# Even mixer of a two-block network: pool products in the first attention step, four output slots woven into the attention, a room of its own for the fourth one's weights

## What is computed

```python
def even_mixer(h, w_in, w_out, q_g, k_g, pool_w, pool_scale):
    proj = h @ w_in
    q, k, v, qi, ki, wi, u = jnp.split(proj, offsets, axis=-1)
    q = rms_norm_2(q.reshape(b, t, A_HEADS, HEAD_DIM), q_g)
    k = rms_norm_2(k.reshape(b, t, A_KV_HEADS, HEAD_DIM), k_g)
    attn = dsa_attention(q, k, v, qi, ki, wi)      # 8 heads, each query sees 64 chosen keys
    pooled = multiscale_pool(u, pool_w, pool_scale)
    return jnp.concatenate([attn, pooled], axis=-1) @ w_out

def multiscale_pool(u, pool_w, pool_scale):        # 4 groups of 128 features, windows 2, 4, 8, 16
    for g, w in enumerate(POOL_WINDOWS):
        outs.append((hi - lo) / count - groups[:, :, g])   # mean of the last w tokens, less the token
    y = jnp.einsum('btgc,gcd->btgd', mixed, pool_w)
    return y * pool_scale
```

## Time and profile before

| | |
|---|---|
| median of 3 runs | 1366.63 us (1365.58 to 1368.62) |
| the profiled execution's own time | 1366.33 us |
| its span, first to last instruction | 1364.5 us |
| PE busy | 1313.2 us, 96% of the span |
| PE weight load, DVE, ACT, POOL busy | 1262.1, 667.7, 676.8, 1017.6 us |
| mean granted clock of TensorE | 0.990 |
| share of PE in the chain that ended last | 79% |

### The profile page before, as it was taken

The page is one execution under the profiler, slowest core; times in us unless marked ns, Lnnn a source line. Parts: engine busy times, 40 slices in busy tenths (PEclk is TensorE's granted clock), DMA queues, the critical chain, the costliest instruction groups (busy, mean ns, idle before and its releaser), DMA issues.

```text
span 1364.5 us, 27769 instructions
## 1 busy us (share of the span) xinstructions
PE 1313.2 (96%) x11024; PEld 1262.1 (92%) x11024; DVE 667.7 (49%) x1168; ACT 676.8 (50%) x933; POOL 1017.6 (75%) x794
## 2 busy tenths in 40 slices
PE   7989999999999989999999979999999999999999
PEld 6879999999988889999999858999999998999999
DVE  8994465555556757555566484211113545211112
ACT  7715543444666656444456545444445445544442
POOL 1226898888777549888887775988887764888885
PEclk9989999999999989999999989999999999999999
DMA  6313675555544334555554532555554432555530
GB/s 261 125 63 126 180 245 186 183 179 180 167 149 161 110 108 163 185 184 180 179 178 144 186 123 68 208 180 179 181 179 159 152 124 93 173 189 181 180 141 31
DMA packets 33879, 217.07 MB, mean 159 GB/s; under 512 B 3683, under 2 KB 7428, under 8 KB 8196
## 3 DMA queue, kind: packets, MB, share of 16 engines
q1 hardware_dynamic: 30096, 211.14, 43.9%
q10 hardware_dynamic: 3700, 4.75, 1.4%
HBM read 213.26 MB, written 2.62 MB: 158 GB/s over the span
## 4 chain that ended last, share of the span: by engine, by line
PE 79%; DVE 11%; ACT 4%; issue 2%; POOL 2%; DMA 1%; DVEq 0%; ACTq 0%; SPq 0%; POOLq 0%
PE up L1481 18%; PE up L1482 17%; PE up L1483 17%; PE acc L1481 6%; PE acc L1483 6%; PE acc L1482 6%; PE up L1601 2%; POOL w_lo L380 1%; ACT w_hi L461 1%; DVE opnd L877 1%; DVE s_work L1017 1%; DVE mix L886 1%; PE side L1687 1%; DVE s_work L1026 1%; DVE mix L1359 0%
## 5 line engine op out<-in xcount | busy, mean ns | idle before, releaser
L380 POOL TENSOR_TENSOR w_lo<-ring,w_hi 128x512 fp32r<-128x512 f32 x756 | 974.0, 1322 | 241.4 <-ACT w_hi L461 238.4
L1481 PE MATMUL up<-opnd,w_hi 128*128 128x256 f32 x2128 | 613.7, 288 | 12.6 <-DVE opnd L1401 3.1
L1482 PE MATMUL up<-opnd,w_lo 128*128 128x256 f32 x2128 | 604.0, 284 | 0.0
L1483 PE MATMUL up<-opnd,w_hi 128*128 128x256 f32 x2128 | 603.9, 284 | 0.0
L461 ACT ACTIVATE w_hi<-ring 128x2048 fp32r<-128x2048 f32 x191 | 364.6, 1910 | 263.7 <-PE up L1483 210.0
L1481 PEld LDWEIGHTS up<-opnd,w_hi 128*128 128x128 f32 x2128 | 409.7, 193 | 26.8 <-issue 20.1
L1482 PEld LDWEIGHTS up<-opnd,w_lo 128*128 128x128 f32 x2128 | 410.2, 193 | 1.3 <-issue 1.0
L1483 PEld LDWEIGHTS up<-opnd,w_hi 128*128 128x128 f32 x2128 | 410.1, 193 | 0.0
L1481 PE MATMUL acc<-opnd,w_hi 128*128 128x256 f32 x768 | 218.4, 284 | 2.5 <-DVE opnd L1118 2.5
L1482 PE MATMUL acc<-opnd,w_lo 128*128 128x256 f32 x768 | 218.0, 284 | 0.0
L1483 PE MATMUL acc<-opnd,w_hi 128*128 128x256 f32 x768 | 218.0, 284 | 0.0
(11 more groups left out here) (267 smaller groups left out, 1396.0 us busy)
## 6 DMA issues: line engine op xcount, KB each, us to landing
ring<-in_stream SPq DMA_DIRECT2D x197, 1024.0 KB, 4.8
bias_rows<-mix ACTq DMA_DIRECT2D x1, 1536.0 KB
mix<-in_s_b SPq DMA_DIRECT2D x1, 1024.0 KB, 5.6
...
```

Of the source, the lines that this page charges most:

```text
L380: ins = nc.gpsimd.tensor_tensor(w_l[:, cols], ring[:, r, cols], w_h[:, cols].bitcast(f32), ALU.subtract)
L1481: MM(o, l_hi, r_hi, start=start, stop=False, skip_group_check=True)
L1482: MM(o, l_lo, r_hi, start=False, stop=False, skip_group_check=True)
L1483: return MM(o, l_hi, r_lo, start=False, stop=stop, skip_group_check=True)
```

## The change

- The negated pool weights `e_pwn` are written once by ACT. PE multiplies them with u in step 0, as soon as u is there, and adds the products of the weights with the means (sum x 1/count) in the same banks: pool_w x (mean - u) is formed in PSUM. POOL's subtraction L441 goes, and each of its four multiplications tells PE that it is done. The second part of the products stands in step 0 too, in place of step 2.
- ACT and DVE make the pieces 4 to 7 of the operand in step 1 (before: step 3 on ACT, steps 3 and 4 on DVE).
- `fill` starts in step 2 and holds all four slots. The fourth slot uses bank 0 of `acc` once all scores are read: its pieces 4 to 7 in steps 9 and 10, 0 to 3 at the end of step 12. `slot_part` looks up the weights' places, `residual` takes a table of banks.
- The fourth slot's weights get other places in `mix`: over the index vectors and raw queries (high) and over u (low). ACT writes the high part in step 4 (before: step 9), and that of output slot 2 behind the first exponentials (before: ahead of the loop).

```diff
--- before.py
+++ after.py
@@ -295,8 +295,8 @@
         (k_k, k_q, k_v, k_mask, k_tri, k_z, k_t, k_b, k_a, k_out) = carve(
             (KT, T), (KT, T), (TT, D), (384,), (P,), (3, 768), (2, 768), (2, 768), (2, 768), (2, T))
 
-        last_hi = {START["wo"] + 3: mix_r[:, 0:2048], START["evout"] + 3: mix_r[:, 512:2560]}
-        last_lo = {START["wo"] + 3: mix_r[:, 6144:8192], START["evout"] + 3: mix_r[:, 2560:4608]}
+        last_hi = {START["wo"] + 3: mix_r[:, 0:2048], START["evout"] + 3: mix_r[:, 1536:3584]}
+        last_lo = {START["wo"] + 3: mix_r[:, 6144:8192], START["evout"] + 3: mix_r[:, 11984:14032]}
 
         def weights_hi(s):
 
@@ -305,6 +305,8 @@
         def weights_lo(s):
 
             return last_lo[s] if s in last_lo else w_lo[:, s % SPLIT]
+
+        e_pwn = e_at[:, 0].rearrange("p (g d) -> p g d", g=4)
 
         def heads(v):
 
@@ -436,9 +438,7 @@
             pool.wait_ge(dma["causal"], 48)
             for g in range(4):
                 c.up(nc.gpsimd.tensor_tensor(e_cnt[:, g], e_cnt[:, g], (e_pa if g % 2 else e_pb)[:, g, 16:], ALU.mult),
-                     "pool_step")
-            pool.wait_ge(sem("pool_step"), c.of("pool_step").value())
-            c.up(nc.gpsimd.tensor_tensor(e_cnt, e_cnt, e_u[:, :, 16:], ALU.subtract), "pooled")
+                     "pooled")
             low_parts(START["evout"], N_SLOTS)
 
 
@@ -455,7 +455,7 @@
                 if s == START["wo"] + 3:
                     act.wait_ge(sem("diff_scores"), HEADS)
                 elif s == START["evout"] + 3:
-                    act.wait_ge(sem("scores"), 8)
+                    act.wait_ge(sem("qk_ready"), 8 + 3)
                 elif s >= START["glu"] + SPLIT:
                     act.wait_ge(sem("mm_done"), dyn * RING + (s - SPLIT + 1))
                 c.up(A(weights_hi(s), ring[:, s % RING], ACT.Copy), "w_hi_ready")
@@ -806,14 +806,15 @@
             index_relu(0)
             high_parts_to(S + 5)
             index_relu(1)
+            act.wait_ge(dma["causal"], 48)
+            c.up(A(e_pwn, e_pw, ACT.Copy, scale=-1.0), "pool_neg")
             high_parts_to(S + 8)
             even_square(1)
             even_root(1)
             even_square(2)
-            high_parts_to(S + 9)
             for n in range(EVEN_STEPS):
-                if n == 3:
-                    c.wait("pool_ps", 4)
+                if n == 1:
+                    c.wait("pool_ps")
                     for m in range(4):
                         c.up(A(hi("mixed")[:, 4 + m], up[(BANK["evout"] + m // 2) % 2][:, m % 2], ACT.Copy,
                                scale=pcol("pscale", m, 1)), "hi_ready")
@@ -821,13 +822,15 @@
                     even_probs_copy(n - 2)
                 if n < 8:
                     softmax_exp(n, e_l, e_st)
+                if n == 0:
+                    high_parts_to(S + 9)
                 if n == 1:
                     even_root(2)
                 if n >= 5 and n % 2:
                     h = (n - 5) // 2
                     c.wait("pv")
                     c.up(A(hi("mixed")[:, h], aux[h % 2][:, 0:T], ACT.Copy), "hi_ready")
-                if n == 9:
+                if n == 4:
                     high_parts_to(S + 10)
             residual("ffn2", START["evout"], lead=3)
 
@@ -1182,12 +1185,12 @@
                 low_tile(end, 7)
                 c.tell("mix_free")
 
-            def residual(name, S, u0, third=None):
+            def residual(name, S, u0, own={}):
                 for g in range(4):
                     dve.wait_ge(sem("mm_done"), S + g + 1)
                     for e in range(2):
                         m = 2 * g + e
-                        o = third[:, e * T:e * T + T] if third is not None and g == 2 else up[(u0 + g) % 2][:, e]
+                        o = own[g][:, e * T:e * T + T] if g in own else up[(u0 + g) % 2][:, e]
                         c.up_and_wait(V.tensor_tensor(x[:, m], x[:, m], o, ALU.add), "x_ready")
                     c.tell("up_free")
                     for e in range(2):
@@ -1305,7 +1308,7 @@
                     c.wait("hi_ready")
                     c.up(V.scalar_tensor_tensor(lo("diff")[:, h], sq[:, h], sub_g, hi("diff")[:, h].bitcast(f32),
                                                 ALU.mult, ALU.subtract), "lo_ready")
-            residual("ffn1", START["wo"], BANK["wo"], acc[:, 3])
+            residual("ffn1", START["wo"], BANK["wo"], {2: acc[:, 3]})
 
             pe_operand()
             ffn(1, "ple1")
@@ -1395,9 +1398,9 @@
                     softmax_tail(n - 1, e_l, e_a, e_st, False)
                 if n == 2:
                     even_normed(2)
-                if n in (3, 4):
-                    c.wait("hi_ready", 2)
-                    for m in (2 * n - 6, 2 * n - 5):
+                if n == 1:
+                    c.wait("hi_ready", 4)
+                    for m in range(4):
                         c.up(V.scalar_tensor_tensor(lo("mixed")[:, 4 + m], up[(BANK["evout"] + m // 2) % 2][:, m % 2],
                                                     pcol("pscale", m, 1), hi("mixed")[:, 4 + m].bitcast(f32),
                                                     ALU.mult, ALU.subtract), "lo_ready")
@@ -1406,7 +1409,7 @@
                     c.wait("hi_ready")
                     c.up(V.tensor_tensor(lo("mixed")[:, h], aux[h % 2][:, 0:T], hi("mixed")[:, h].bitcast(f32),
                                          ALU.subtract), "lo_ready")
-            residual("ffn2", START["evout"], BANK["evout"], acc[:, 3])
+            residual("ffn2", START["evout"], BANK["evout"], {2: acc[:, 3], 3: acc[:, 0]})
 
             ffn(2, "odd")
             c.tell("mix_free")
@@ -1537,14 +1540,14 @@
 
             def slot_part(name, s, o, ks, fresh=True, order=range(KT)):
 
-                b = s % SPLIT
+                w_h, w_l = weights_hi(s), weights_lo(s)
                 for k in ks:
                     if fresh:
                         c.wait("hi_ready")
                         c.wait("lo_ready")
                     for m in range(2):
                         w = slice((2 * k + m) * P, (2 * k + m + 1) * P)
-                        ins = three(o[:, m], w_hi[:, b, w], w_lo[:, b, w], hi(name)[:, k], lo(name)[:, k],
+                        ins = three(o[:, m], w_h[:, w], w_l[:, w], hi(name)[:, k], lo(name)[:, k],
                                     k == order[0] and m == 0, k == order[-1])
                 if ks[-1] == order[-1]:
                     c.up(ins, "mm_done")
@@ -1963,9 +1966,19 @@
                 c.up(ins, "pv")
 
             out = START["evout"]
-            fill = {4: [(0, [4, 5])], 5: [(0, [6, 7])], 6: [(1, [4, 5])], 7: [(1, [6, 7])], 8: [(0, [0]), (1, [0])],
-                    9: [(2, [4, 5, 6, 7])], 10: [(0, [1]), (1, [1]), (2, [0, 1])], 11: [(0, [2]), (1, [2]), (2, [2])],
-                    12: [(0, [3]), (1, [3]), (2, [3])]}
+            fill = {2: [(0, [4, 5, 6, 7])], 3: [(1, [4, 5])], 4: [(1, [6, 7])], 5: [(2, [4, 5])], 6: [(2, [6, 7])],
+                    7: [(0, [0]), (1, [0]), (2, [0])], 9: [(0, [1]), (1, [1]), (2, [1]), (3, [4, 5])],
+                    10: [(3, [6, 7])], 11: [(0, [2]), (1, [2]), (2, [2])],
+                    12: [(0, [3]), (1, [3]), (2, [3]), (3, [0, 1, 2, 3])]}
+            banks = {}
+
+            def pool_part(weights, v, first):
+
+                for m in range(4):
+                    ins = MM(banks[m // 2][:, m % 2], weights[:, m], v(m), start=(first and m % 2 == 0), stop=not first,
+                             skip_group_check=True)
+                return ins
+
             for n in range(EVEN_STEPS):
                 if n < 8:
                     even_scores(n)
@@ -1976,21 +1989,24 @@
                             pe.wait_ge(sem("lo_ready"), KT * UNIT["mixed"] + 2 * g + 2)
                         if g == 2:
                             used[0] += 1
-                            banks.append(acc[:, 3].rearrange("p (a t) -> p a t", a=2))
+                            banks[g] = acc[:, 3].rearrange("p (a t) -> p a t", a=2)
+                        if g == 3:
+                            used[0] += 1
+                            pe.wait_ge(sem("scores_read"), 8)
+                            banks[g] = acc[:, 0].rearrange("p (a t) -> p a t", a=2)
                     slot_part("mixed", out + g, banks[g], ks, fresh=(g == 0), order=MIXED_ORDER)
                 if n == 0:
+                    banks = {0: bank(), 1: bank()}
+                    pe.wait_ge(sem("pool_in"), 2)
+                    c.wait("pool_neg")
+                    pool_part(e_pwn, lambda m: e_u[:, m, 16:], True)
                     even_stats(2)
+                    c.wait("pooled", 4)
+                    c.up(pool_part(e_pw, lambda m: e_cnt[:, m], False), "pool_ps")
                 if 2 <= n < 10:
                     even_transposes(n - 2)
                 if 4 <= n <= 10 and n % 2 == 0:
                     even_values((n - 4) // 2)
-                if n == 2:
-                    banks = [bank(), bank()]
```

(5 more changed lines are left out.)

## The result

| | before | changed |
|---|---|---|
| median of 7 runs each, side by side | 1364.70 us | 1369.10 us (1368.69 to 1370.80) |
| ratio, 95% interval | | 1.0027 (1.0017 to 1.0037) |
| the profiled execution, its span | 1366.33, 1364.5 us | 1368.78, 1367.0 us |

The change costs 3.7 us by the ratio (2.3 to 5.0 by its interval), more than the 0.2% that can be told from nothing. The forecast was +4.2 us and 1370.5 us. (The base alone covers the 1.4 us between 1370.5 and 1369.1: the forecast started from 1366.33, and the median of the seven runs beside the changed kernel is 1364.70.) The ratios here are of fast runs alone; one run of the kernel before, beside e1, e3, e4 and e5, took 1937.97 us at a granted clock of 0.606 and is in none of them.

A forecast was written before the change was run, and what follows sets the result against it. PE is 96% busy, but a chain off PE sets ffn2's start at T0 + 9.4 us. Terms 2.9 + 1.7 + 0.35 - 2.4 = +2.55 us for T0, +4.25 with the clock behind it: 1370.5 us, range 1365.5 to 1374.

The forecast's parts named there:

- T0: Moment when output slot 0 is complete, 835.5 in the earlier trace; forecast to move +2.55 us, to about 838.
- chain from T0 to ffn2: Additions, operand tiles, ACT's high part and POOL's low part fix ffn2's start at T0 + 9.4 us, whatever PE does.
- Paid in full: Work moved ahead of T0 on PE costs its whole time; work behind T0 is free.
- Term 1: 24 of the fourth slot's 48 matmuls move ahead of T0: +2.9 us; PE then stands still about 4.9 us before ffn2.
- Term 2: Input term on PE, four more fp32 products in step 0: +1.7 us; POOL's dropped 2.69 us released nobody in time.
- Terms 3 and 4: PE's waits from scores 0 to the first pieces, then on to T0: 8.5 us for 8.15, +0.35 us.
- The wait of 3.2 us: PE's first pieces of slot 0 wait for the first low part of the pooled tiles, from 801.3 to 804.5.
- Term 5: POOL's low part of the fourth slot blocks DVE's tails 4 and 5; without it T0 would come about 1 us earlier.
- Rival D: Tails 4 and 5 blocked more, PE feels 2 us, low clock behind T0 twice as long: about 1374; chance 0.13.
- Term 6: Clock ahead of T0: one low stretch costing 0.9 us replaces two costing 3.3, so -2.4 us.
- Term 7: Clock behind T0: a low stretch on ffn2's first slot after PE's 4.9 us gap, +1.7 us (bounds 0 and 3.3).
- C: Rival: DVE catches up in steps 1 to 7 as POOL finishes low parts 2.7 us sooner; 1363.5, chance 0.09.

The follow-up runs named there:

- e1: Changed kernel with all eight pieces of the fourth output slot at the end of step 12, none in steps 9 and 10; ratio 0.9997 to the kernel before.
- e3: Kernel before, with a bank of its own for the fourth output slot and no work moved; ratio 1.0003 to the kernel before.
- e4: e3 plus own places for the weights of ffn2's first slot, converted during the attention; ratio 0.9983 to the kernel before.
- e5: Changed kernel plus own places for the weights of ffn2's first slot, converted in step 9; ratio 0.9991 to the kernel before.
- e11: e9 with the input term on PE, negated products in step 0, pooled ones in step 1, no POOL subtraction; ratio 0.9964 to the kernel before.
- e2: Changed kernel with the input term back on POOL, four pool products in step 0 instead of eight; ratio 1.0002 to the kernel before.
- e6: e1 with ACT writing the fourth slot's high part in step 8 instead of step 4; ratio 0.9978 to the kernel before.
- e9: Changed kernel with input term on POOL, products in step 1, pieces spread thinner, fourth slot last, its high part in step 8; ratio 0.9963 to kernel before.
- e8: e9 plus own places for the weights of ffn2's first slot, high part in step 9; ratio 0.9956 to the kernel before.
- e12: e8 with the high parts of the fourth slot and ffn2's first slot in steps 6 and 8, not 8 and 9; 1356.89 us, ratio 0.9937.

## Why the prediction was right, point by point

- **What bounds the section** was read rightly. The chain from T0 to ffn2 has kept its length (9.30, 9.23 us), and removing the bank's wait is worth nothing (e3). When the chain is cut, ffn2 moves forward (e4, e5). "Paid in full" was too strong: work ahead of T0 that fills a wait is paid in part (terms 1 and 2) or not at all (e11).
- **Term 1, the fourth slot's matmuls**: predicted +2.9 and a gap of about 4.9 us; the gap is 4.96. e1 undoes it and wins 1.9 us at T0. It was 1 us too high, as the pieces also cover 0.75 us of another wait.
- **Term 2, the input term**: predicted 1.7 us on PE. The products take 1.8 us from start to start (791.78 to 793.58). Scores 1 are 5.30 us behind scores 0 and were 2.56, so 2.74 later; predicted 2.7. But the step counted the whole term as the price of having it on PE. With it on POOL (e2) 1.0 of the 1.8 is spent waiting.
- **Terms 3 and 4, the waits**: predicted 8.5 us in all. Measured 0.32 + 0.80 + 2.93 + 0.27 + 1.35 + 0.84 + 1.25 = 7.76. The wait of 3.2 us came with 2.93, those in front of k = 0, transposes 6 and k = 1 with 1.35, 0.84 and 1.25. The wait of scores 4 for the logits did not come; transposes 4 waited 0.27 us in its place.
- **Term 5, DVE under POOL**: right; 1.4, 1.2 and 1.3 us for three operations, about 1.5 us of PE's path (e6). Rival D's trigger was there; its price, 2 us more than the forecast, wasn't.
- **Term 6, the clock ahead of T0, is the step that failed in the profiled run.** Predicted -2.4 us: one low stretch of 3.3 us, partly over a wait. The low stretches of the changed kernel, against the earlier trace rows (the last one is ffn2's first slot):

```profile
799.80:806.60 6.80, 5.42 (x25) 5.45 (x26) 6.62 (x11) 0.95 (x2) 6.55 (x6) 0.50 0.56 202
827.10:830.50 3.40, 3.40 (x16) 3.40 (x17) 0.00 (x0) 0.00 (x0) 0.00 (x0) 0.50 0.02 5
847.60:851.00 3.40, 3.40 (x18) 3.40 (x18) 3.03 (x5) 2.64 (x6) 3.40 (x3) 0.50 0.69 234
```

  The clock fell while PE still stood in the gap of 2.93 us and stayed low for 6.8 us, 5.4 of them over PE's work. The 24 matmuls of slot 0 took 806.44 - 801.18 = 5.26 us instead of 2.9. A second stretch followed at 827.1. In these two PE lost 2.4 us and 0.44 x 3.4 = 1.5, together 3.9. The two of before (the windows of the earlier trace rows start up to 0.7 us late; the stretches themselves, at a clock of 0.50, run from 801.0 to 804.4 and from 811.3 to 814.7) lost 1.4 on the pool products (3.19 us for what takes 1.8 in the changed kernel) and 1.5, together 2.9. So it is about +1.0 in the place of -2.4, and T0 moved by 5.6 us instead of 2.55. Without the clock the terms hold: 2.9 + 1.8 - 0.2 for the waits behind the start of scores 0 (7.95 to 7.76), 4.5, where the prediction had 4.95. The trace of before could have warned of it, for it has a low stretch of 6.8 us outside the section, from 497.2 to 504.0, with PE busy for 6.06 us of it.
- **Term 7, the clock behind T0**: predicted +1.7, measured 8.19 - 6.69 = +1.5.

In this pair of traces the section therefore moved by 7.0 us and not by 4.25, and the whole launch by 2.5. That the ratio gives 3.7 so near to the forecast is in part luck, with a clock term that came out 3.4 us off where it could be seen.

Over many runs the clock agrees better with the prediction's net (-2.4 + 1.7 = -0.7 us). The mean granted clock of the seven runs of the changed kernel is 0.9900; the kernel before has 0.9890, 0.9896 and 0.9898 in three sets of 34, 22 and 12 runs. A thousandth is 1.4 us, so the net over the whole launch is between -0.3 and -1.4. This is weak evidence: none of these sets is the seven runs beside the changed kernel, and a mean over the launch doesn't say what fell into this section. The terms of work and waits were right within 0.5 us in sum; where the clock goes is not shown over many runs.

**What was not forecast, and is open.** C, the rival on the other side, stayed away: of the four tail operations of steps 0 and 1 three take 1.19, 1.18 and 1.25 us (DVE L1226, L1227), like those of the earlier trace rows, for POOL went straight on to its twelve low parts at 791.45. How the 3.7 us divide between the weaving and the input term is not settled by the ratios: e1 gives about 4 us to the weaving, e2 about 3 to the term, each good to 2 us or so on either side, and the two are more than the whole. The traces give about 1 us to the term, and to the weaving 1.9 ahead of T0 and 1.5 behind it (the clock on ffn2's first slot), together 4.4. The clock is the likely reason for the rest: the mean granted clocks are 0.9910 in e1 and 0.9920 in e2 against 0.9900, worth 1.4 and 2.7 us. A kernel with both undone and the rest kept was not run (e9 changes the order too), so it stays open.

The same holds for the gains. The mean granted clock over all runs of each is 0.9889 in e3, 0.9887 in e4, 0.9907 in e5, 0.9925 in e6, 0.9931 in e9, 0.9918 in e8, 0.9930 in e12 and 0.9907 in e11, with 0.9890 to 0.9898 for the kernel before. So up to 4.8 of e9's 5 us, and up to 4.4 of e12's 8.6, stand in the clock. One low stretch less in the section, 1.7 us, is part of that; for the rest no run shows whether the order or chance brought it.
